# A two-block transformer kernel: smaller first pieces in the head, tokens before context in the first key chunk, and steps moved between chunks

## What is computed

```
m = silu(c) @ w_mod + b_mod                     # shift, scale, gate ...
hx, hc = x * (1 + sc1) + sh1, ctx * (1 + csc1) + csh1
q = rope(hx @ Wq);  k = [hc @ Wk, rope(hx @ Wk)];  v = [hc @ Wv, hx @ Wv]
p = softmax(q0 k0) - lam * softmax(q1 k1)       # two maps per head, 8 heads
x = LN(ALPHA * x + g1 * (rms(p v) * g) @ Wo)
x = LN(ALPHA * x + g2 * swiglu(modulate(x)))
```

## Time and profile before

| | |
|---|---|
| three executions | 1099.7, 1099.9, 1099.97 us; median 1099.9 |
| the profiled execution | 1099.21 us |
| its span, first to last instruction | 1097.5 us |
| TensorE busy (products) | 1084.3 us, 5814 products |
| VectorE, ScalarE busy | 772.5 us, 584.7 us |
| moved from HBM | 237 MB, 218 GB/s over the span |
| granted TensorE clock, mean | 0.998 of 2.4 GHz |

### The profile page before, as it was taken

How to read it: one execution, slowest core, us unless ns; L and a number is a source line. 1 busy time by engine, 2 the same in 40 slices (tenths; PEclk the granted TensorE clock), 3 DMA queues, 4 the chain that set the end, 5 groups by cost and what they waited for, 6 DMA issues and landing times.

```text
span 1097.5 us, 14415 instructions
## 1 busy us (share of the span) xinstructions
PE 1084.3 (99%) x5814; PEld 904.0 (82%) x5814; DVE 772.5 (70%) x1006; ACT 584.7 (53%) x823; POOL 63.0 (6%) x121
## 2 busy tenths in 40 slices
PE   8999999999999999999999999999999999999998
PEld 4798766899998877888888778887888888888886
DVE  2597598889799797976745855455657667785445
ACT  3742376563444356655544667455765366563343
POOL 0012200002121101000000000000000000000000
PEclk9999999999999999999999999999999999999999
DMA  9997840679999966678567788877534446555542
GB/s 363 403 332 260 250 146 1 211 258 346 373 375 351 351 217 208 219 245 282 197 212 130 219 179 179 171 166 149 162 115 154 154 153 230 169 215 192 192 154 77
DMA packets 112418, 240.40 MB, mean 219 GB/s; under 512 B 5760, under 2 KB 52224, under 8 KB 110816
## 3 DMA queue, kind: packets, MB, share of 16 engines
q1 hardware_dynamic: 97152, 184.37, 53.8%
q0 software_dynamic: 14912, 54.86, 13.9%
q10 hardware_dynamic: 288, 0.26, 0.1%
HBM read 237.34 MB, written 2.12 MB: 218 GB/s over the span
## 4 chain that ended last, share of the span: by engine, by line
PE 86%; DVE 8%; DMA 4%; ACT 1%; issue 1%; SPq 0%; DVEq 0%; ACTq 0%
PE ps L2082 18%; PE ps L2084 17%; PE ps L2083 17%; PE ps L2150 10%; PE ps L2152 5%; DVE wL L1234 3%; PE ps L2117 2%; PE ps L2119 2%; PE ps L2118 2%; PE ps L2267 2%; DVE modraw L1310 2%; PE ps L2399 1%; PE ps L2367 1%; DMA raw<-in_ffn_w_in 1%; DMA modraw<-in_mod_rows 1%; DMA raw<-in_w_in 1%
## 5 line engine op out<-in xcount | busy, mean ns | idle before, releaser
L1234 DVE TENSOR_TENSOR wL<-raw,wH 128x1024 fp32r<-128x1024 f32 x324 | 392.1, 1222 | 202.0 <-ACT wH L653 200.0
L653 ACT ACTIVATE wH<-raw 128x1024 fp32r<-128x1024 f32 x324 | 337.0, 1057 | 291.8 <-PE ps L2084 180.3
L2082 PE MATMUL ps<-wH,aHL 128*128 128x512 f32 x576 | 229.0, 398 | 0.4 <-issue 0.3
L2083 PE MATMUL ps<-wL,aHL 128*128 128x512 f32 (+1 forms) x592 | 229.0, 387 | 0.0
L2084 PE MATMUL ps<-wH,aHL 128*128 128x512 f32 x576 | 224.6, 390 | 0.0
L2150 PE MATMUL ps<-aHL,wH 128*128 128x512 f32 x480 | 167.1, 395 | 0.0
L2152 PE MATMUL ps<-aHL,wL 128*128 128x256 f32 x480 | 133.1, 277 | 0.0
L2082 PEld LDWEIGHTS ps<-wH,aHL 128*128 128x128 f32 x576 | 108.2, 188 | 29.7 <-issue 6.9
L2083 PEld LDWEIGHTS ps<-wL,aHL 128*128 128x128 f32 x592 | 111.3, 188 | 21.4 <-issue 0.5
L2084 PEld LDWEIGHTS ps<-wH,aHL 128*128 128x128 f32 x576 | 108.1, 188 | 23.2
L2150 PEld LDWEIGHTS ps<-aHL,wH 128*128 128x128 f32 x480 | 90.0, 188 | 20.8
(11 more groups left out here) (326 smaller groups left out, 1477.8 us busy)
## 6 DMA issues: line engine op xcount, KB each, us to landing
raw<-in_ffn_w_in SPq DMA_DIRECT2D x88, 512.0 KB
modraw<-in_mod_rows POOLq DMA_DIRECT2D x80, 512.0 KB, 6.8
raw<-in_w_in SPq DMA_DIRECT2D x32, 1024.0 KB
raw<-in_ffn_w_out SPq DMA_DIRECT2D x22, 1024.0 KB
raw<-in_w_up SPq DMA_DIRECT2D x16, 1024.0 KB
raw<-in_w_down SPq DMA_DIRECT2D x16, 1024.0 KB
mod<-in_mod_first SPq DMA_DIRECT2D x8, 1024.0 KB, 16.6
raw<-in_attn_w_qkv SPq DMA_DIRECT2D x8, 1024.0 KB
```

Source lines behind the costliest of these rows:

```text
L653: nc.scalar.activation(wHigh(n), raw[:, (n // 2) % RAW, (n % 2) * 1024:(n % 2) * 1024 + 1024], ACT.Copy).then_inc(w_hi, 1)
L1234: V.tensor_tensor(wL[:, n % WL, :], raw[:, (n // 2) % RAW, (n % 2) * 1024:(n % 2) * 1024 + 1024], wHigh(n).bitcast(fp32), ALU.subtract).th ...
L2082: T.matmul(outp, xh, h, start=first, stop=False, skip_group_check=part_of)
L2083: T.matmul(outp, xh, l, start=False, stop=False, skip_group_check=part_of)
```

## The change

- **Head in eighths.** The first block's columns are laid out in two halves of 128 columns (with all rows), each one 1 MB transfer. SP loads the first half, the first query sub-chunk, x, the second half, the second sub-chunk. `mod_mm_half`, `mod_select_half`, `mod_put_half` and `hi_x(..., ks=(e,))` work on one half, which serves one row block of x. The first six products of q_mm(0, 0) follow the first half, then come the second half block, six products of q_mm(1, 0) and the other six of q_mm(0, 0). There are 2 + 1 + 1 zero products instead of 3. In the rounds s = 1 and 2 one part of q_mm(1, s) moves ahead of `mod_mm`, one stays between it and the selection, and two follow. All counts of `mod_out` and `mod_acc` grow by one (`NMODS`).
- **Key chunk.** In chunk 2 the token unit comes before the context unit; the context tokens are loaded between the two key pieces; banks are dealt out accordingly. scores(3) waits for one unit of v less.
- **Steps.** Of the 24 modulation steps, 7, 5, 7 and 5 beside the chunks 2 to 5 become 4, 6, 8 and 6.
- **wo's last sub-chunk** is converted after the attention loop: on ScalarE ahead of square(2), on VectorE after normed(1, 1) (`adv(SUBS["wo"] + WS - 1)` between `normed(1, 1)` and `vec_put(1)`).
- **Three orders.** The gate product of chunk 10 follows two conversions instead of three. `residual_1` takes both gate products of tile 1 before its sums. At (15, 2) of the win stage `beside` comes before `adv` on both engines.

```diff
@@ -100,12 +101,12 @@
-QKV_STEPS = {(c, j): ((2, 2, 1, 2), (2, 1, 1, 1), (2, 2, 2, 1), (1, 2, 2, 0))[c - 2][j] for c in range(2, 6) for j in range(4)}
+QKV_STEPS = {(c, j): ((1, 1, 1, 1), (2, 2, 1, 1), (2, 2, 2, 2), (2, 2, 2, 0))[c - 2][j] for c in range(2, 6) for j in range(4)}
...
-QKV_BANK = (0, 2, 6, 0, 2, 6, 0, 2, 6, 0)
-QKV_FREE = (0, 0, 0, 1, 2, 3, 4, 5, 6, 7)
+QKV_BANK = (0, 2, 0, 6, 2, 0, 6, 2, 0, 6)
+QKV_FREE = (0, 0, 1, 0, 2, 3, 4, 5, 6, 7)
@@ -473,14 +474,26 @@
             for m in range(NMOD0):
+                if m == 0:
+                    sp.dma_start(mod0[:, 0, :], a["mod_first"][:, 0, 0, :]).then_inc(mod0_in[0], 16)
+                    sp.dma_start(raw[:, 0, 0:D], a["qkv_first"][:, 0, 0, :]).then_inc(q_first[0], 16)
+                    sp.dma_start(xT[:, 0:2, :], a["x_cols"][:, 0:2, :]).then_inc(x_in[0], 16)
+                    sp.dma_start(mod0[:, 1, :], a["mod_first"][:, 0, 1, :]).then_inc(mod0_in[1], 16)
+                    sp.dma_start(raw[:, 0, D:2 * D], a["qkv_first"][:, 0, 1, :]).then_inc(w_raw[0], 32)
+                    continue
...
                 sp.dma_start(raw[:, m, D:2 * D], a["qkv_first"][:, m, 1, :]).then_inc(w_raw[m], 32)
-            sp.dma_start(ctxT, a["ctx_cols"]).then_inc(ctx_in, 16)
+            keys = by_k(a["attn_w_qkv"][0])[:, :, 2 * CW:3 * CW]
             for c in range(2, 6):
-                chunk(SUBS["qkv"] + 4 * c, a["attn_w_qkv"][0], c * CW)
+                if c == 2:
+                    piece(SUBS["qkv"] + 8, [((0, CW), keys[:, 0:4, :])])
+                    sp.dma_start(ctxT, a["ctx_cols"]).then_inc(ctx_in, 16)
+                    piece(SUBS["qkv"] + 10, [((0, CW), keys[:, 4:8, :])])
+                else:
+                    chunk(SUBS["qkv"] + 4 * c, a["attn_w_qkv"][0], c * CW)
@@ -713,10 +727,10 @@
                 .then_inc(cT_ready, 1)
-            def hi_x(c, shift, scale):
+            def hi_x(c, shift, scale, ks=range(2)):
                 act.wait_ge(x_in[c], 16)
-                for k in range(2):
+                for k in ks:
@@ -737,12 +751,18 @@
             mc = modulated(0, 0, 0)
-            for c in range(NMOD0):
-                if c:
-                    act.wait_ge(mod_sel, c)
-                mod_copy(c)
+            for e in range(2):
+                if e:
+                    act.wait_ge(mod_sel, 1)
+                mod_copy(e)
+                adv(e)
+                act.wait_ge(mod_out, e + 1)
+                hi_x(0, *mc(0), ks=(e,))
+            for c in range(1, NMOD0):
+                act.wait_ge(mod_sel, c + 1)
+                mod_copy(c + 1)
                 adv(2 * c)
-                act.wait_ge(mod_out, c + 1)
+                act.wait_ge(mod_out, c + 2)
@@ -846,10 +866,9 @@
                     square((r - 5) // 4)
-                elif r == 2:
-                    adv(SUBS["wo"] + WS - 1)
...
                 hi_t("o", j, gain=subg)
+            adv(SUBS["wo"] + WS - 1)
@@ -1131,6 +1150,10 @@
                 for j in range(3):
+                    if (c, j) == (15, 2):
+                        beside(c, j)
+                        adv(n + 4 * c + WS + j)
+                        continue
@@ -1286,9 +1309,18 @@
+            def mod_put_half(e):
...
+                dve.wait_ge(mod_sel, e + 1)
+                for w in range(2):
+                    ins = V.scalar_tensor_tensor(
+                        out=modcol[:, 0, w, e, :], in0=ps[:, 7, 4 * w + 2 * e:4 * w + 2 * e + 2], scalar=float(w),
+                        in1=bcol[:, 8 * w + e:8 * w + e + 1].to_broadcast([P, 2]), op0=ALU.add, op1=ALU.add)
+                ins.then_inc(mod_out, 1)
...
-                dve.wait_ge(mod_sel, c + 1)
+                dve.wait_ge(mod_sel, c + 2)
@@ -1325,13 +1357,21 @@
             dve.wait_ge(cT_ready, 2)
-            for c in range(NMOD0):
+            def low_x(c, k):
...
+                dve.wait_ge(xq_hi, 2 * c + k + 1)
+                V.tensor_tensor(aL[:, 2 * c + k, :], tf[:, c % 2, k * S:(k + 1) * S],
+                                aH[:, 2 * c + k, :].bitcast(fp32), ALU.subtract).then_inc(xq_lo, 1)
...
+            for e in range(2):
+                mod_put_half(e)
+                adv(e)
+                low_x(0, e)
+            for c in range(1, NMOD0):
...
                 for k in range(2):
-                    dve.wait_ge(xq_hi, 2 * c + k + 1)
-                    V.tensor_tensor(aL[:, 2 * c + k, :], tf[:, c % 2, k * S:(k + 1) * S],
-                                    aH[:, 2 * c + k, :].bitcast(fp32), ALU.subtract).then_inc(xq_lo, 1)
+                    low_x(c, k)
@@ -1457,8 +1497,6 @@
                     maxima(r + 2)
-                if r == 3:
-                    adv(SUBS["wo"] + WS - 1)
@@ -1559,6 +1598,26 @@
+                def product_part(t, b):
+                    cols = slice(b * CW, (b + 1) * CW)
+                    if b == 0:
+                        dve.wait_ge(half_done, t + 1)
+                    else:
+                        product_done("out0", t)
+                    return V.tensor_tensor(lnt[:, b, :], pair(un + t)[:, b, :], g2b0[:, cols], ALU.mult)
...
+                def residual_1():
+                    product_part(1, 0)
+                    adv(first + 3)
+                    product_part(1, 1).then_inc(acc_out, 1)
+                    dve.wait_ge(acc_out, un + 2)
+                    for b in range(2):
+                        cols = slice(b * CW, (b + 1) * CW)
+                        link(V.scalar_tensor_tensor(out=x[:, 1, cols], in0=x[:, 1, cols], scalar=ALPHA,
+                                                    in1=lnt[:, b, :], op0=ALU.mult, op1=ALU.add))
+                        V.bn_stats(bn[:, 1, 6 * b:6 * b + 6], x[:, 1, cols]).then_inc(dve_self, 1)
+                        links[0] += 1
@@ -1649,7 +1708,7 @@
                 hidden(0, full)
-                residual(1)
+                residual_1()
@@ -1745,7 +1804,8 @@
                         return
-                    for j in range(3):
+                    early = (0, 1) if layer == 0 and c == 10 else (0, 1, 2)
+                    for j in early:
@@ -1756,6 +1816,8 @@
                     V.tensor_tensor(hid[:, c % 2, :, :], sil[:, c % 2, :, :], other, ALU.mult).then_inc(acc_out, 1)
+                    if len(early) == 2:
+                        adv(n + 4 * c + WS + 2)
@@ -1967,6 +2029,10 @@
                 for j in range(4):
+                    if (c, j) == (15, 2):
+                        moba_beside(c, j)
+                        adv(n + 4 * c + WS + j)
+                        continue
@@ -2087,13 +2153,13 @@
                     sub_ready(n + s)
-                    if t_need is not None:
-                        pe.wait_ge(t_need, s + 1)
                     for un, (xh, xl) in zip(units, acts):
+                        if t_need is not None and un == UNITS["k"]:
+                            pe.wait_ge(t_need, s + 1)
...
                             at_least(pe, acc_out, QKV_FREE[un] if un < UNITS["wo"] else un - 1)
-                            if un == UNITS["k"]:
-                                pe.wait_ge(mod_out, NMOD0)
+                            if un == UNITS["k"] + 1:
+                                pe.wait_ge(mod_out, NMODS)
@@ -2283,6 +2349,24 @@
+            def mod_mm_half(e):
...
+                pe.wait_ge(mod0_in[e], 16)
+                for h in range(2):
+                    for j in range(4):
+                        k0 = (4 * h + j) * 256
+                        ins = T.matmul(ps[32 * j:32 * j + 32, 6, 0:256], cT[:, 4 * h + j, :], mod0[:, e, k0:k0 + 256],
+                                       start=h == 0, stop=h == 1)
+                ins.then_inc(mod_acc, 1)
...
+            def mod_select_half(e):
...
+                pe.wait_ge(mod_row, e + 1)
+                for w in range(2):
+                    ins = T.matmul(ps[:, 7, 4 * w + 2 * e:4 * w + 2 * e + 2], modrow[:, w * P:(w + 1) * P],
+                                   cst[:, C_SELC:C_SELC + 2], start=True, stop=True)
+                ins.then_inc(mod_sel, 1)
@@ -2294,9 +2378,8 @@
-                pe.wait_ge(mod_row, c + 1)
-                if c:
-                    pe.wait_ge(mod_out, c)
+                pe.wait_ge(mod_row, c + 2)
+                pe.wait_ge(mod_out, c + 1)
@@ -2329,21 +2412,29 @@
-            mod_mm(0)
+            mod_mm_half(0)
             pe.wait_ge(cst_in, 16)
-            mod_select(0)
-            zero_mm(3, 5)
-            q_mm(0, 0)
+            mod_select_half(0)
+            zero_mm(2, 5)
+            q_mm(0, 0, range(2))
+            mod_mm_half(1)
+            pe.wait_ge(mod_out, 1)
+            mod_select_half(1)
+            zero_mm(1, 5)
+            q_mm(1, 0, range(2))
+            q_mm(0, 0, range(2, 4))
             mod_mm(1)
-            q_mm(1, 0, range(1))
+            q_mm(1, 0, range(2, 3))
             mod_select(1)
-            q_mm(1, 0, range(1, 4))
+            q_mm(1, 0, range(3, 4))
+            zero_mm(1, 5)
...
                 q_mm(0, s)
```

(24 more changed lines are left out.)

2 lines of the change are left out of this document (1 added, 1 removed).

## The result

The kernel after takes 1100.8 us (median of 20 executions, 1099.6 to 1103.3), the kernel before 1099.6 beside it (20 executions). The ratio is 1.0013, with a 95% interval of 1.0007 to 1.0019: **+1.4 us**. I had forecast 0.5 us less; the value lies inside my range, the sign was wrong. The profiled execution of after is the slowest of the 20: 1103.32 us, span 1101.6. So its profile holds some 2.5 us that a usual execution does not.

A forecast was written before the change was run, and what follows sets the result against it. TensorE, busy 99% of the span, was taken as the bound. Head +1.7, attention -1.0 and repairs -0.3, -0.3, -0.6 summed to -0.5 us: 1098.7 us for the profiled execution, 1099.4 on the median's scale, range 1097.5 to 1102.2.

The forecast's parts named there:

- The head: Start of the kernel, first block in eighths: early start worth nothing, later rounds lose; +1.7 us, bounds +1.1 and +3.2.
- The two rounds: Later head rounds: only six products cover the fixed chain, so each takes 9.3 instead of 8.63 us; +1.36 together.
- the start of the first full block: Head: the block starts at 19.2 instead of 18.94 us; +0.3, bounds -0.25 and +1.0.
- The landing that I set against a quicker head: Second weight piece lands near 18.6 us, against the rival of a winning head (1097.0 us, chance 0.03).
- The key chunk: Tokens before context: same 144 products, the later context load covered by token products; 0, bounds 0 and +0.5 us.
- The steps: Modulation steps moved between chunks: nothing won or lost on TensorE; 0, bounds 0 and +0.4 us.
- Attention: Scores stop waiting for v's second copy and wo's late conversion, 0.5 us each; -1.0, bounds -0.4 and -1.5.
- The rival that attention opens further: VectorE's relief also removes the waits in attention's tail: gain 3.0 instead of 1.0 us, 1097.4 us; chance 0.06.
- Residual: Second gate product of tile 1 ahead of the first half's sum removes a 0.38 us wait; -0.3, bounds -0.6 and 0.
- Gate product: Chunk 10: ahead of one conversion, removing a 0.57 us wait, half returning at the last conversion; -0.3, bounds -0.7 and 0.
- oa: Chunk 15: swapped with a conversion, its low parts come 1.2 us earlier, removing a 0.43 us wait; -0.6, bounds -0.3 and -0.7.
- The clock rival: Head, hole from 12.6 to 16.4 us: TensorE drops to the 1.2 GHz level; +2.8 us, 1102.2 us; chance 0.10.

The follow-up runs named there:

- e6: The kernel after with the order of the rounds s = 1 and 2 of before; 1098.9 us, ratio 0.9996 to the kernel before.
- e2: The kernel before with tokens first in the key chunk, new banks, one unit of v less to wait for and wo's late conversion; 1097.4 us, ratio 0.9980.
- e3: The kernel before with only the modulation steps changed from 7, 5, 7, 5 to 4, 6, 8, 6; 1099.1 us, ratio 0.9998.
- e5: The kernel after with the head of before (whole first block, old order of the rounds); 1097.3 us, ratio 0.9983 to the kernel before.
- e11: The kernel after with the head of before, the pool's scale loaded behind the modulation rows and the first exponential ahead of a conversion; 1095.9 us, ratio 0.9969.
- e7: The kernel before with only the gate product of chunk 10 moved ahead of one conversion; 1100.3 us, ratio 1.0006.
- e9: The kernel after with the 512 KB pool's scale issued on POOL's queue behind the modulation row of step 71; 1100.1 us, ratio 1.0002 to the kernel before.

## Why the prediction was wrong, point by point

**The head: +1.7 predicted, +3.0 in the kernel after.** The two rounds were right in mechanism and in size: 9.3 long, with waits of 0.46 ahead, 1.37 us by e6 where the sum had 1.36. The step that failed is the start of the first full block, "+0.3": measured 20.01 against 18.07 at a full clock. Two things are in it. First, the second eighth does not run from its landing alone. Its weights were in at 12.5 as assumed, but the half block stands in TensorE's order behind the six products that had waited for x (issued at 1.72, landed 8.2 us later, behind two weights in the queue), began at 13.23 and was followed by four handovers; the products came at 17.07, not 16.4. From 13.23 on the chain took 3.84 us, where the sum had 3.9, so the handovers were priced rightly. What was missing is TensorE's own order, 0.7 us ahead of the chain; the upper bound of 1.0 was about large enough for it, for another reason. Second, the reference point was bad: 18.94 came from an execution with a granted clock of 0.70 early on, which e2, e3 and e5 do not show. I had that row in hand, used it for a rival, and did not ask where TensorE would stand without it.

The landing that I set against a quicker head was read wrongly too. "At best the block moves by 0.25 us" takes the second piece, in at 18.6, as the time when the block may start. But the first half of the block's products use the first piece, in at 3.5+12.7 = 16.2, and the second is needed only half a block, some 0.9 us, after the start. So the landings allowed a start at about 17.7, and e5 shows one ahead of 18.6, with no gap inside:

```profile
18.07 1.92 PE L2326 MATMUL ps<-mod,cT 128*32 128x512 f32 x16
```

So the landing did not hold the block; the chain of the second eighth did (17.07, and twelve products behind it).

**The key chunk: 0 predicted.** Its cover was named, the floor was not. In the order of before the first key piece's landing and the context's chain behind it hold the key chunk at 47.5 to 48.0, and tokens first is worth 0.7 to 1 us (e2). In the kernel after the head arrives at 49.8, too late to use it. So 0 is what the change shows, and the potential gain was spent on the slower head: the parts alone do not add up to the whole.

**The steps: 0** was right (e3).

**Attention: -1.0 predicted, -1.18** measured, of which the two waits named are 2.19-1.65 = 0.54 for v and 3.04-2.59 = 0.45 for the exponential, by the distances between the scores; 0.19 is spread over later loops. Nothing was late behind the moved conversion. This step was right. The rival that attention opens further did not happen: the waits in its tail, 1.0 for am and 0.9 for at, are the same in before, after and e11.

**Three repairs: -1.2 predicted.** Residual: -0.33 against -0.3. Gate product: -0.3 predicted with "half of that should return as wait at its last conversion"; more than all returned, +0.7 by the median of e7 (interval -0.7 to +1.9), 1.1 to 2.2 us at the last conversion. The direction of that warning was right and its size was not: I took VectorE for the chain there, and did not look at the transfer that VectorE waits for, which sets the time of the last conversion whatever is gained ahead of it. oa: -0.6 predicted, 0 measured: I named no next waiter, and there was one 5 us behind, ScalarE's conversion and table load ahead of the exponential.

**The sum** as measured: +3.0 for the head less 0.7 to 1 by the floor removed, -1.2 attention, -0.3 residual, about +0.7 gate, 0 oa and steps: +1.2 to +1.5, beside +1.4. The gate's term is the weakest of them, because its interval holds 0; by the excesses it is +0.4 in e7 and +1.4 in the profiled execution of after, the slowest of its 20. The measurement was also finer than the 2.2 us that I gave it: its interval is 1.3 us wide, and that is why a change of +1.4 can be told from none.

**The clock rival** did not happen at its place: the granted clock of after is 1.00 from 10 to 15 and from 15 to 20 us in spite of the holes, so the hole between the first products and the second column chunk cost no clock. It fell elsewhere, behind the 2.03 us wait at 385:

```profile
10.00:15.00 5.00, 3.28 (x25) 1.54 (x23) 0.70 (x2) 1.59 (x4) 0.00 (x0) 1.00 1.01 415
15.00:20.00 5.00, 4.43 (x18) 2.85 (x18) 1.78 (x4) 1.77 (x3) 0.00 (x0) 1.00 1.01 417
...
388.40:391.40 3.00, 3.00 (x8) 2.31 (x7) 3.00 (x4) 2.51 (x3) 0.00 (x0) 0.50 0.99 403
```

The columns are those of the earlier trace rows; 0.50 is the 1.2 GHz level. In e5, with 1.37 us of waiting at the same place, the products behind it are 0.23 apart and the granted clock is 1.00.

## What to carry to other kernels

Before a part is made faster, find the floor that holds the next part (here the landing of the first key piece and the conversions behind it): it hides gains and losses ahead of it, and lifting it changes what the part is worth. Before a wait of TensorE is repaired, find who waits next behind the same engine, and see whether the wait is there in more than one execution. Where the engine that is late waits for a transfer, look first at what stands ahead of that transfer in its own queue: moving one 512 KB load back took away the longest wait.

## What was not expected of the hardware

In the trace of after a single wait of 2.03 us between dense products was followed by a granted clock of 0.50 for 3 us, at a price of 1.4 us on top; behind 1.37 us in e5 it did not fall. This is one trace of each. The first 15 us of one and the same head ran at a mean granted clock of 0.68 to 0.70 between 10 and 15 us in three of nine traces and at 1.00 in six, with the first product 0.35 to 0.64 us later. And a transfer's time from issue to use in POOL's queue went from 13.8 to 7.9 us (issued 359.47, used 373.24 in after; issued 359.26, used 367.18 in e9) by one 512 KB transfer less ahead of it, more than the 1.3 us that 512 KB take at the 415 GB/s which all queues moved together in the head.
